# The first two layers of a four-layer transformer kernel: block-sparse attention merged with the output products, its preparation set beside the input products

## What is computed

```python
outs = jnp.stack([
    short_conv_mixer(a_h, a_b, a_c, conv_w),                                     # group 0
    nsa_mixer(n_q, n_kv, n_g, positions, cmp_pos, cmp_w1, cmp_w2),               # group 1
    gla_mixer(l_q, l_k, l_v, l_g, l_lr, gla_gate_w2, gla_gate_b),                # group 2
    gmlp_mixer(m_u, m_v, gmlp_ws, gmlp_b),                                       # group 3
], axis=2)
outs = rms_norm(outs, grp_gain.reshape(N_MIXERS, GROUP_WIDTH))
return outs.reshape(B, S, D_MODEL) @ w_o
# nsa_mixer: k, v of 32-token windows are compressed by a two-layer net (cmp_w1 2048x128, cmp_w2);
# o = g0 * softmax(q kc') vc + g1 * softmax(rot(q) rot(k_slc)') v_slc + g2 * softmax(rot(q) rot(k_win)') v_win
```

## Time and profile before

| | |
|---|---|
| median of 3 runs | 1677.92 us (1675.04 to 5094.15; the last is one disturbed execution) |
| profiled execution | 1681.13 us, span of its records 1679.40 us |
| TensorE matmul busy | 1529.5 us (91%), weight loads 1489.0 us |
| VectorE, ScalarE, POOL busy | 1106.8, 757.7, 397.8 us |
| mean granted clock of TensorE | 0.926 of full speed |
| bytes over DMA | 336.69 MB, mean 200 GB/s |

### The profile page before, as it was taken

One profiled execution on the slowest core, in us unless ns is written; L12 is line 12 of the kernel. 1 busy time (PEld: TensorE's weight loads), 2 busy tenths in 40 slices (PEclk: granted clock), 3 DMA queues, 4 the chain that ended last, 5 costly groups with the idle time before them and its releaser, 6 DMA issues. The chain is left out here.

```text
span 1679.4 us, 28072 instructions
## 1 busy us (share of the span) xinstructions
PE 1529.5 (91%) x11950; PEld 1489.0 (89%) x11950; DVE 1106.8 (66%) x1491; ACT 757.7 (45%) x1016; POOL 397.8 (24%) x369
## 2 busy tenths in 40 slices
PE   3898689999898689999899787999999998999998
PEld 3886579999887489999899687999999996999998
DVE  7874758699455549779675655777449763556554
ACT  3533445533562536543487323444335443344432
POOL 0000302099000022069200212200227800401022
PEclk7997769999799779999799897999999999989999
DMA  9760549789241127879454002577546771536550
GB/s 394 305 226 1 188 170 372 301 317 345 100 170 55 75 101 273 343 289 344 156 192 160 1 1 100 199 296 291 218 151 253 274 284 68 189 139 238 213 201 26
DMA packets 47213, 336.69 MB, mean 200 GB/s; under 512 B 5361, under 2 KB 5745, under 8 KB 6769
## 3 DMA queue, kind: packets, MB, share of 16 engines
q1 hardware_dynamic: 46224, 333.03, 53.1%
q10 hardware_dynamic: 864, 1.87, 0.3%
HBM read 333.83 MB, written 1.05 MB: 199 GB/s over the span
## 5 line engine op out<-in xcount | busy, mean ns | idle before, releaser
L424 DVE TENSOR_TENSOR weights_hi_lo<-ring,weights_hi_lo 128x1024 fp32r<-128x1024 f32 x426 | 554.8, 1325 | 299.1 <-ACT weights_hi_lo L417 297.9
L417 ACT ACTIVATE weights_hi_lo<-ring 128x1024 fp32r<-128x1024 f32 x426 | 445.7, 1058 | 545.9 <-PE PS L529 295.0
L529 PE MATMUL PS<-hi,weights_hi_lo 128*128 128x256 f32 x3200 | 522.8, 286 | 19.0 <-ACT hi L644 12.1
L529 PEld LDWEIGHTS PS<-hi,weights_hi_lo 128*128 128x128 f32 x3200 | 448.0, 194 | 21.5 <-issue 19.4
L812 PE MATMUL PS<-acts_hi_lo,weights_hi_lo 128*128 128x256 f32 x3552 | 437.6, 286 | 22.4 <-DVE weights_hi_lo L424 11.6
L812 PEld LDWEIGHTS PS<-acts_hi_lo,weights_hi_lo 128*128 128x128 f32 x3552 | 433.5, 193 | 26.8 <-POOL acts_hi_lo L757 14.3
L755 POOL CAST acts_hi_lo<-arena 128x256 fp32r<-128x256 f32 x148 | 133.2, 900 | 843.3 <-PE PS L812 424.6
L529 PE MATMUL PS<-lo,weights_hi_lo 128*128 128x256 f32 x1600 | 325.0, 285 | 0.0
L435 DVE CUSTOM_DVE_ANT_0 ring<-ring,cond 128x1024 f32<-128x1024 f32 x192 | 256.4, 1374 | 0.0
L529 PEld LDWEIGHTS PS<-lo,weights_hi_lo 128*128 128x128 f32 x1600 | 251.7, 193 | 0.0
L529 PE MATMUL PS<-weights_hi_lo,hi 128*128 128x256 f32 x1248 | 203.7, 285 | 3.5 <-DVE weights_hi_lo L424 2.2
(11 more groups left out here) (339 smaller groups left out, 1084.5 us busy)
## 6 DMA issues: line engine op xcount, KB each, us to landing
ring<-in_stream_dram SPq DMA_DIRECT2D x313, 1024.0 KB, 4.9
constS<-in_const_dram SPq DMA_DIRECT2D x1, 1856.0 KB, 11.9
cond<-in_rows_dram SPq DMA_DIRECT2D x2, 512.0 KB, 6.0
arena<-in_x_dram ACTq DMA_DIRECT2D x1, 1024.0 KB, 12.1
smallS<-in_small_dram SPq DMA_DIRECT2D x1, 883.0 KB, 12.8
out_dram<-arena ACTq DMA_DIRECT2D x2, 256.0 KB, 2.4
out_dram<-arena SPq DMA_DIRECT2D x2, 256.0 KB, 2.8
constS<-in_const_dram SPq DMA_DIRECT2D x1, 320.0 KB, 14.1
```

Source lines behind the costliest of these rows:

```text
L417: act.activation(wsp[:, g % 2, 0, at:at + HALF], ring[:, n % RING, at:at + HALF], ACT.Copy).then_inc(*ready.one())
L424: dve.tensor_tensor(wsp[:, g % 2, 1, at:at + HALF], ring[:, n % RING, at:at + HALF], wsp[:, g % 2, 0, at:at + HALF].bitcast(F32), ALU.subt ...
L529: mm = pe.matmul(o, lhs, rhs, start=k + g + j == 0, stop=k == KD - 1 and j == 2, skip_group_check=True)
```

## The change

- **Slots.** In proj the q slot and the key slot move from places 9 and 10 to 4 and 5. The two cmp slots stand behind these products in the stream, and TensorE multiplies them between input products. The output weights come in the order of groups 2, 3, 0, 1. Mod 4 of layer 0 moves from out to proj: 12 mod slots beside 12 products instead of 8.
- **Proj.** `nsa_inputs` runs beside it: POOL builds the compression's input (`blocks`) and does the rotation (`rotation`, 13 instructions one after another), TensorE compresses and transposes q, k, ScalarE copies. The proj phase uses PSUM banks 0 to 2 instead of 0 to 3. The scratch for this lies in `later` and in the place of constants that are not loaded yet, so `later_inputs` moves to layer 1 and waits there for the attention.
- **`nsa_out_phase`** replaces phases 2 and 3 and three quarters of phase 4, in one block with its neighbours: attention, each group's norm (sums with a column of ones; root, reciprocal and spread by TensorE in place of the 512-column product with logarithm and exponential), and the output products of groups 2, 3 and 0 in between. The group of the attention comes last; its output product is the only slot left in the out phase, and adds to the tiles (`fresh=False`).
- Layers 0, 1 and the proj of layer 2 stand in one block.

The core of the diff (the sources of `nsa_phase` and `group_norm_phase` are deleted whole; their instructions return in the new functions unless said otherwise):

```diff
-        groups = (("lk", "lr"), ("kc", "vc", "lq"), ("mv",), ("lv",), ("mu",), ("lg",), ("ah",), ("ac",), ("ab",),
-                  ("q",), ("ks", "ks", "kw", "kw"), ("vs", "vw", "ng"))
+        groups = (("lk", "lr"), ("kc", "vc", "lq"), ("mv",), ("lv",), ("q",), ("ks", "ks", "kw", "kw"), ("mu",), ("lg",),
+                  ("ah",), ("ac",), ("ab",), ("vs", "vw", "ng"))
...
     if kind == "proj" and l == 0:
-        return [2, 3]
-    if kind == "out" and l == 0:
-        return [4]
+        return [2, 3, 4]
...
+            proj[at[5] + 1:at[5] + 1] = [("cmp", ("cmp", l, 1))]
+            proj[at[4] + 1:at[4] + 1] = [("cmp", ("cmp", l, 0))]
...
+            def rotation(pool, order):
+                pool.wait_ge(*taken.at(6))
+                order(pool.tensor_copy(QKR, QK))
+                for m in range(TT):
...
+                    for sign, a, b2, o in ((ALU.subtract, 0, 8, 0), (ALU.add, 8, 0, 8)):
+                        order(pool.tensor_tensor(t1, x[:, :, a:a + 8], cos, ALU.mult))
+                        order(pool.tensor_tensor(t2, x[:, :, b2:b2 + 8], sin, ALU.mult))
+                        ins = pool.tensor_tensor(y[:, :, o:o + 8], t1, t2, sign)
...
+            def pe_beside(pe):
+                for i in range(12):
+                    if i in (4, 5):
...
+                        for r in range(16):
+                            q = 16 * j + r
+                            mm = pe.matmul(PS[0:32, 3, 0:P], zT[:, q, :], w1[:, r, :], start=q == 0, stop=q == 31)
+                        mm.then_inc(used["pe"], 1)
...
@@ nsa_out_phase, TensorE
+                scores(0)
+                scores(1)
+                pe.wait_ge(*mixed["banks"])
+                scores(2)
+                scores(3)
...
+                for i in range(3):
+                    mm = sums(i, 2, 2 * i, i == 0)
+                mm.then_inc(*gsum.one())
+                for r in range(4, 8):
+                    scores(r)
+                pe.wait_ge(*grc.at(1))
+                spread_group(0, 2, 0, True)
+                spread_group(1, 2, 256, False)
+                turn_probs(1)
+                pe.wait_ge(*sd.at(1))
+                turn_probs(2)
+                pe.wait_ge(*wt.at(8))
+                for g in range(2):
+                    rows_half(pe, slots[0], g, y_of, fresh=True)
+                turned_taken(pe, 1)
+                turn_probs(0)
...
+                turn_cmp(0, 0)
+                pe.wait_ge(*on.at(4))
+                spread_group(2, 2, 0, True)
...
+                turn_cmp(1, 3)
...
+                turn_probs(4)
...
+                turn_probs(5)
...
+                turn_probs(3)
...
+                pe.wait_ge(*ready["gate"])
+                attend(0, 0)
+                pe.wait_ge(*on.at(6))
+                attend(1, 2)
+                rows_half(pe, slots[1], 0, y_of, fresh=False)
+                pe.wait_ge(*fin.at(1))
+                transposes(pe, lambda i: O[:, i % 2, i // 2 * P:i // 2 * P + P], 4, 3, ft)
+                rows_half(pe, slots[1], 1, y_of, fresh=False)
+                rows_half(pe, slots[2], 0, y_of, fresh=False)
+                sums(3, 0, 0, True).then_inc(*gsum.one())
+                rows_half(pe, slots[2], 1, y_of, fresh=False)
+                pe.wait_ge(*grc.at(2))
+                spread_group(3, 2, 0, True)
...
@@ nsa_out_phase, VectorE
+                dve.wait_ge(multiplied.sem, product_no[slots[0]])
+                scores_masked(0)
+                scores_masked(1)
+                row_max(0, 1)
+                scores_masked(2)
+                scores_masked(3)
+                row_max(0, 0)
...
+                dve.reciprocal(gr[:, 0:6], gr[:, 0:6]).then_inc(*grc.one())
+                scores_masked(4)
+                scores_masked(5)
+                row_max(1, 1)
+                normed(0, 2, 0)
+                scores_masked(6)
+                scores_masked(7)
+                row_max(1, 0)
...
+                dve.wait_ge(*grt.at(2))
+                dve.reciprocal(gr[:, 6:8], gr[:, 6:8]).then_inc(*grc.one())
+                for n in following:
+                    split_lo(dve, n)
+                normed(3, 2, 0)
...
         with block() as blk:
             start_phase(blk)
-            layers[0][0](blk)
+            for l in range(2):
+                inputs, mixers, mixed = layers[l]
+                inputs(blk)
+                mixers(blk)
+                outputs(blk, l, mixed, acts_ready=state.pop("mixed"), fresh=False)
+                if l == 1:
+                    later_inputs(blk)
+                ffn_phases(blk, l)
```

More of the change, by code:

```diff
@@ L21 @@
 NEG = -1e30
+STOP = object()
 SLOT = 2048
@@ L60, in out_slots @@
     name, i, chunks = {"mix": ("w_o", l, 8), "hyb": ("hyb_w_out_2", 0, 8), "ret": ("ret_w_out_2", 0, 16)}[kind]
-    return [("rows", name, i, k, 0) for k in range(0, chunks, 2)]
+    return [("rows", name, i, k, 0) for k in ((4, 6, 0, 2) if kind == "mix" else range(0, chunks, 2))]
 def up_slots(l):
@@ L458, in slots_of @@
             mod, todo, seen = mods_beside(name), [], 0
+            state["cmp"] = [n0 + d for d, (what, _) in enumerate(items) if what == "cmp"]
             for d, (what, _) in enumerate(items):
+                if what == "cmp":
+                    continue
                 if what == "mod":
@@ L499, in _ @@
                 load_weights(sp)
-                if name == ("proj", 0):
-                    sp.wait_ge(sig("layer0_inputs").sem, 32)
             @blk.tensor
@@ L758, in split_acts, with rows_half, rows_gemm_phase @@
                                        ALU.subtract).then_inc(*acts_lo.one())
-        def rows_gemm_phase(blk, name, l, lhs, half, acts_split=0, acts_ready=None, next_norm=None):
+        def rows_half(pe, n, g, y_of, fresh):
+            w_hi, w_lo = halves_of(n, "rows")
+            a = rows_no[n]
+            a_hi, a_lo = asp[:, a % 2, 0, :, :], asp[:, a % 2, 1, :, :]
+            pe.wait_ge(acts_lo.sem, 2 * a + g + 1)
+            if g:
+                pe.wait_ge(used["dve"], ordinal[n][1])
+            else:
+                pe.wait_ge(half_lo_ready.sem, product_no[n] + 1)
+            for k in range(KD):
+                for j, (w, x) in enumerate(pieces(w_hi, w_lo, a_hi, a_lo)):
+                    mm = pe.matmul(y_of(k), w[:, g, k * P:(k + 1) * P], x[:, g, :],
+                                   start=fresh and g + j == 0 and (k % 2 == 0 or k == KD - 1), stop=False, skip_group_check=True)
+            mm.then_inc(*(multiplied if g else half_multiplied).one())
+        def rows_gemm_phase(blk, name, l, lhs, half, acts_split=0, acts_ready=None, next_norm=None, fresh=True):
             split_before = state["split"]
@@ L966, in short_mixers @@
-        def short_mixers(l, convT, lqT, lkT, lrT, LV, LG, MU, MV, oT):
+                nsa_pe, nsa_act, blocks, rotation = nsa_inputs(l, kvcT, QK, VN)
+                pe, act, dve, pool = short_mixers(l, convT, lqT, lkT, lrT, LV, LG, MU, MV, oT, blocks, rotation)
+                gemm_phase(blk, ("proj", l), token_major, evac, banks=3, split_weights=True,
+                           beside=(side_by_side(pe, nsa_pe), side_by_side(act, nsa_act), dve, pool))
+            return proj, lambda blk: nsa_out_phase(blk, l, VN, oT), oT[:, 2:4, :]
@@ L974, in short_mixers @@
+        def short_mixers(l, convT, lqT, lkT, lrT, LV, LG, MU, MV, oT, blocks, rotation):
             S = 8192
@@ L1528, in mixers @@
                 hyb_mixers(Q, GT, SQ, oT, S)
-            return proj, mixers, None, oT
+            return proj, mixers, oT
         ST = {n: 64 + 8 * i for i, n in enumerate(("g", "beta", "gc", "glast", "eg", "ed", "beg", "t0", "t1"))}
@@ L2212, in build, with _ @@
                     second_condition(blk)
+            layers[2][0](blk)
+            @blk.sync
+            def _(sp):
+                sp.wait_ge(sig("layer2_inputs").sem, 32)
+        for l in range(2, len(LAYERS)):
+            _, mixers, mixed = layers[l]
+            mixers()
+            with block() as blk:
+                outputs(blk, l, mixed)
+                ffn_phases(blk, l)
                 if l + 1 < len(LAYERS):
```

675 lines of the change are left out of this document (373 added, 302 removed).

## The result

The changed kernel takes **1628.95 us** (median of 4 runs, 1624.11 to 1630.09) where the kernel before takes 1677.68 (median of 4): ratio **0.9709, 95% interval 0.9682 to 0.9736**. The forecast was 1639, range 1620 to 1664. In two later series, each of 6 runs beside the kernel before on the same chip, the changed kernel had 1624.24 us (0.9699, interval 0.9671 to 0.9726) and 1627.99 us (0.9699, interval 0.9672 to 0.9726).

A forecast was written before the change was run, and what follows sets the result against it. TensorE, busy 91% of the span, was taken as the bound. Layer 0 was to go from 188.9 to 161.7 us and layer 1 from 174.8 to 160.0, together minus 42.0 from 1681.1: 1639, range 1620 to 1664.

The forecast's parts named there:

- The waits before products 5 and 6: Input products: compression placed there gives VectorE 7 us, removing TensorE waits of 5.1 (layer 0) and about 2.2 us (layer 1).
- Rival 2: Layer 0's proj: POOL and VectorE hinder each other, VectorE has 105 us instead of 82, 11 longer; 1650 us; chance 0.07.
- lead: Merged stage, from the last input product to the first output product: 14 us, on VectorE, at 2.4 GHz.
- The allowance: Merged stage: 7.9 us for lost clock on top of 60.2 at 2.4 GHz, taken together as 68 per layer.
- The 2.3 us behind the lead: Merged stage: clock loss expected in the products after the lightly busy start, 2.3 us.
- the values, given half of 5.2: Merged stage: clock loss for handoffs between, half of the 5.2 or 0 us that the old value products lost.
- 3.6 us gap: Layer 0: a gap after which 12.4 us ran at clock 0.76, taken as 3.0 us lost before the last slot.
- 1: Merged stage stretched by TensorE's fixed order, late probability copies or masks holding output products: 71 to 85 us; chance 0.30.
- 3: Both merged stages at half clock throughout: 107 us each, 1717 in total, slower than before; chance 0.03.
- 4: Little of the merged stage overlaps, only block borders and compression are won: stage about 88 us, total 1679; chance 0.05.
- the rule: Merged stage: waits between bursts throttle TensorE to half rate repeatedly; by it the stage goes to its half-clock end, time 1717.
- no change from layer 0's up on: Sign of being right: everything from layer 0's up onward stays as before, outside the changed proj and merged stages.

The follow-up runs named there:

- preparation_behind: Changed kernel with TensorE's and ScalarE's attention preparation (compression, transposes and copies of q, k) behind the last input product instead of between products: 1650.76 us, ratio 0.9823.
- mod4_alone: Kernel before with only layer 0's mod 4 moved from out to proj: 1674.60 us, ratio 0.9973.
- after_again: The changed kernel itself, unchanged, run and profiled a second time: 1624.24 us, ratio 0.9699 to the kernel before.

## Why the prediction was right

- **Proj.** Forecast 93.7 and 92.0, measured 91.9 and 94.1. The waits before products 5 and 6 are gone as argued: the compression stands where VectorE was late, and preparation_behind shows the reverse. In layer 0 the mod slot ahead of the second product's low part cost 1.1 instead of 2.0. TensorE's busy time rose by 8.8 us in layer 0 and 11.1 in layer 1, 9.9 in the mean against 9.6 forecast; the two differ by the clock, since the same 576 input products took 73.4 us where they took 74.2 before in layer 0, and 74.3 where they took 72.7 in layer 1. The wait that stays in layer 1 is 2.4, not 1.8.
- **POOL and VectorE in proj.** Both hidden, as said; VectorE 83.6 us busy against 82 forecast. Rival 2 is refuted for proj in its price, not in its mechanism: with the rotation moved away VectorE's splits are 1.2 us shorter in layer 0, where the rival had 23 us for all of POOL's work, and the time is the same. The cost of the mechanism lies in another place: VectorE's split slows POOL ahead of the last slot. The Trainium skill, "SBUF — State Buffer", section "Who interferes with whom", says that a two-input VectorE instruction and a reading GpSimd one exclude each other; the trace now agrees in kind, with 0.40 and 0.74 us alone and 1.39 and 1.6 beside one, and with VectorE's slower split beside POOL.
- **The merged stage.** Forecast 68, measured 67.3 and 67.1. By part, in layer 1: lead 14 forecast, 13.9 measured, ended by VectorE's masks as said. First slot, transposes, compressed branch and values 18.0 at full clock, 22.2 measured, of which the values at half clock are 4.8. Two slots, transposes, sums and POOL's gap 18.3, measured 19.7, with a wait of 5.0 for POOL (4.7 forecast). Last slot 9.9, measured 11.2. The sum at 2.4 GHz was 60.2 and the clock got 7.9; the stage took 6.9 more than 60.2. The allowance was right in size and not in its parts. The 2.3 us behind the lead did not come (clock 0.98 in the second part); the values, given half of 5.2, lost 4.8; behind the gap the last slot lost 1.3, not 3.0. (The 3.6 us gap from which those 3.0 were read stands in layer 0's old out phase, in the row shown with mod4_alone, and not in the earlier trace rows.) And this allowance is the term that another execution moves, so that the forecast met the first profile within 1 us is in part luck: in after_again the stage of layer 0 was shorter by 6.7 us for the same instructions:

```profile
127.63:186.50 58.87, 52.62 (x415) 50.47 (x415) 33.06 (x59) 30.39 (x68) 10.64 (x16) 0.91 0.24 88
```

It runs from the first score to the last output product; the same stretch of the first profile is 65.6 us at clock 0.79.

- **Rivals.** 1, 3 and 4 did not come: no wait for a probability copy or a mask over 1.1 us, and the stage's clock was 0.80 and 0.82. By the rule that the prediction took from the Trainium skill, "TensorE: Matmul & The Clock Gate", section "HAM oscillation — how this bites in real kernels", the stage would have stayed at half rate throughout. In the page's example the waits are longer than the bursts between them; here only POOL's 5.0 us is a long one, and the case that the prediction made of the rule did not come: with full slots between the attention's steps the clock was 0.98 in the second part and 0.93 in the fourth. It fell in parts, and most in the one that has no gap at all, which neither the rule nor the runs explain.
- **The sum.** 42.0 us forecast for the two layers, 43.4 measured in the first profile and 52.6 and 41.9 in the later two. The time itself came 10 us below the 1639 forecast, within the range. The step that was mis-sized is "no change from layer 0's up on", with the norm before it: 2.0 us of waits for the two table loads, which stood in the trace and were not followed when the group norms changed from exponential to root, and 7.3 of clock and small pieces, which the medians show in part (48.7 us between the medians against 52.7 between the profiled executions).

## What to carry to other kernels

When the order of work is what costs, put small dependent steps between large products and the large products between small steps: the attention's preparation in the place of TensorE's waits was worth some 10 us a layer, products within the attention 4 to 5, both with a share of clock that was not parted from the rest. When a function of ScalarE is exchanged, follow its table to the next place that needs one. Take the clock's share from several profiles: one kernel gave 58.9 and 65.6 us for the same stretch. And where a forecast has a term that varies by as much as its error, do not take the match for a proof of the term.

## What the hardware showed beyond that

- The granted clock was 0.50 for 10.3 us in which TensorE was busy without a gap, on 64-column products, and 1.00 for the same 5.4 us of work in another execution of the same kernel.
- POOL's subtraction of 256 columns took 0.74 us alone and 1.6 beside VectorE's weight split, its copy 0.40 and 1.39; VectorE's split half took 1.22 alone and up to 1.76 beside POOL. The whole-execution means of the earlier trace rows, 1.20 and 0.90, are thus means over two situations.
- 32 sums of one column took 6.99 us at half clock where they stood alone behind the attention, and 24 of them 3.80 beside scores.
